# State-space stage: a kernel table padded in device memory, Toeplitz pieces loaded as overlapping rows, half of a table and the late decays moved

## The chip, the cores and the metric

The kernel runs on one core of one Trainium2 chip. The metric is the time of one execution on the device in microseconds (us). The core has TensorE (PE; its weight loads are shown as PEld), VectorE (DVE), ScalarE (ACT), GpSimd (POOL) and SyncE (SP). SP and ACT each have a queue from which they start DMA transfers; all transfers run on 16 DMA engines.

## The reference, cut to what matters

The program is a small encoder: a state-space (S5) layer, a gated MLP, a differential-attention layer, another gated MLP. Only the state-space layer is touched. In each of 64 groups of 16 channels a 64-dimensional complex diagonal state runs over 512 positions:

```python
lb_re, lb_im = mag * jnp.cos(dimg), mag * jnp.sin(dimg)
ht_re = hl_re + pw_re * hp_re - pw_im * hp_im
ht_im = hl_im + pw_re * hp_im + pw_im * hp_re
y = (jnp.einsum("btgp,gcp->btgc", ht_re, cr) - jnp.einsum("btgp,gcp->btgc", ht_im, ci))
y = y + d_skip.astype(f32) * u32
z = jax.nn.gelu(y).astype(u.dtype)
val, gate = jnp.split(z @ w_glu, 2, axis=-1)
return val * jax.nn.sigmoid(gate)
```

## The kernel before

The kernel is written engine by engine: one function for SP, POOL, ACT, DVE and PE each, with semaphores between them, so the order on an engine is the order of the code. The state-space layer splits the 512 positions into 64 blocks (NB) of 8 (BL). The output of a block is a part from within the block, a Toeplitz matrix of the kernel values k[0] to k[7] times the inputs, and a part carried in from the states at the block's start. The work is done in four pieces (OCTS) of 16 groups.

- `kx` holds the kernel values, one row of 8 KB per (piece, input channel), in partitions 32·piece to 32·piece+15. PE computes them in `kernel_rows`, ACT copies them out (L743), POOL adds the skip term to k[0] (L573) and signals `k_ready`.
- `toep[piece]` (1 MB each) holds, in partitions 16·lag to 16·lag+15, the kernel shifted right by 7−lag taps with zeros in front. `load_toeplitz` fills it from SBUF to SBUF with eight DMAs of 16 to 128 KB on SP's queue (L324); the zeros come from POOL's memsets (L571 for pieces 0 and 1, L576 for 2 and 3), which signal `toep_clear`. Pieces 2 and 3 lie where `ada_raw` buffers were, so their memsets wait until all 24 units of `ada_raw` are used (`ada_used`).
- PE's order at the end of the layer is `carried(0)`, `inputs(2)`, three `ada_raw` units, `carried(1)`, `inputs(3)`, `local(0)`, `local(1)`, `back(0)`, `carried(2)`, `local(2)`, `back(1)`, `local(3)`, `back(2)`, `carried(3)`, then the first unit of the gated projection (L2038), `back(3)` in its midst. `local` (L1926) multiplies by `toep`, `carried` (L1941) by the carried states `hx`, `back` (L1952) transposes the activated tile `z`, `inputs` is L1910.
- ACT's order there is `z_steps(0)`, `copy_row(2)`, `z_steps(1)`, `zt_steps(0)`, a weight split, `zt_steps(1)`, `z_steps(2)`, `zt_steps(2)` and so on. `z_steps` (L761) is the gelu of a piece and needs its `local` and `carried`; `zt_steps` (L771) copies what `back` wrote.
- DVE forms `hx` piece by piece: products with the rotation tables `rot_c`, `rot_s`, two scans that read a `decay` tile (L1392, L1393), and six operations that end in L1408, signalling `hx_im`. POOL fills the second half of the rotation tables (L532 to L541) and all four decay tiles (L556, L557).
- SP also issues on the same queue: 24 loads of `ada_raw` (L404, 1 MB each) before the Toeplitz loads, `raw` (L415, the weights of the next stage, 1 MB) after pieces 1 and 3, and `x` (L418, 2 MB).

Of the kernel before, what the change touches and what calls it, by code (L numbers as in the profile page):

```python
# [17 lines left out]
F32 = mybir.dt.float32  # L18
F32R = mybir.dt.float32r
I32 = mybir.dt.int32  # L20
ALU = mybir.AluOpType
ACT = mybir.ActivationFunctionType
AXX = mybir.AxisListType.X

P = 128
D = 1024
SEQ = 512
KT = D // P
# [6 lines left out]
CG = 16  # L35
GROUPS = D // CG
PAIRS = GROUPS // 2
BL = 8
NB = SEQ // BL
OCTS = 4  # L40
PO = PAIRS // OCTS
# [19 lines left out]
N_ADA_PE = 3 * KT  # L61
# [15 lines left out]
def build(nc, a, out_rows):  # L77

    ctx = ExitStack()
    with ctx:  # L80
# [14 lines left out]
        def sem(name):  # L95
            return ctx.enter_context(nc.semaphore(name))
# [3 lines left out]
        raw = at("raw", [P, 2, UNIT], F32, raw_at)  # L100
# [35 lines left out]
        toep = []  # L136
# [14 lines left out]
        for i in range(2):  # L151
# [60 lines left out]

        raw_landed = [sem("raw_landed0"), sem("raw_landed1")]
# [24 lines left out]
        k_psum, k_copied, k_ready, toep_clear = (sem("k_psum"), sem("k_copied"), sem("k_ready"),  # L238
                                                 sem("toep_clear"))
# [80 lines left out]
        def load_toeplitz(eng, piece):  # L320

            eng.wait_ge(toep_clear, piece + 1)
            for lag in range(BL):
                eng.dma_start(toep[piece][CG * lag:CG * (lag + 1), BL - 1 - lag:, :, :],  # L324
                              kx[32 * piece:32 * piece + CG, 0:lag + 1, :, :]).then_inc(toep_in[piece], 16)
# [66 lines left out]
        def _(sp):  # L392
# [17 lines left out]
            for piece in range(OCTS):  # L410
                load_toeplitz(sp, piece)
                if piece % 2:
                    n = piece // 2
                    sp.wait_ge(ada_used, 20 + n)
                    sp.dma_start(raw[:, n, :], a["units"][n]).then_inc(raw_landed[n], 16)  # L415
# [62 lines left out]
        def _(pool):  # L478
# [11 lines left out]
            nc.gpsimd.memset(ones[:], 1.0).then_inc(const_ready, 1)  # L490
            nc.gpsimd.memset(col[:, 0:1], 1.0 / D).then_inc(const_ready, 1)
# [69 lines left out]
            cosines(32, slice(2 * PO, PAIRS), cb[:, 1, :])  # L561
            sines(32, slice(2 * PO, PAIRS), cb[:, 1, :])
            pool.sem_inc(rot_ready, 1)
# [5 lines left out]
            pool.wait_ge(ada_used, 2 * KT)  # L569
            for i in range(2):  # L570
                nc.gpsimd.memset(toep[i][:], 0.0).then_inc(toep_clear, 1)  # L571
            pool.wait_ge(k_copied, 4)
            nc.gpsimd.tensor_tensor(kx[:, 0], kx[:, 0], tk, ALU.add).then_inc(k_ready, 1)  # L573
            for piece in range(2, OCTS):
                pool.wait_ge(ada_used, N_ADA_PE)
                nc.gpsimd.memset(toep[piece][:], 0.0).then_inc(toep_clear, 1)  # L576
                decay_tile(piece)
# [79 lines left out]
        def _(act):  # L657
# [51 lines left out]

            def scaled(piece, quarter):  # L710

                act.wait_ge(u_normed, piece + 1)
                g0 = 2 * PO * piece + 4 * quarter
                for g in range(g0, g0 + 4):
                    ins = A(u[:, g, :], u[:, g, :], ACT.Identity, scale=uab[:, g:g + 1],
                            bias=uab[:, GROUPS + g:GROUPS + g + 1])
                if quarter == 3:
                    ins.then_inc(u_ready, 1)
# [8 lines left out]
            lb_first(3)  # L727
            copy_inputs(2)
# [13 lines left out]
            for b in range(4):  # L742
                A(kx[:, :, 4 * b:4 * b + 4, :].rearrange("p k j c -> p j k c"),  # L743
                  psum[:, 3 + b, :].rearrange("p (j k c) -> p j k c", j=4, k=BL),
                  ACT.Copy).then_inc(k_copied, 1)
            for quarter in range(4):
                scaled(3, quarter)

# [345 lines left out]
        def _(dve):  # L1094
# [570 lines left out]
            dve.wait_ge(pos_in, 16 * BL + 16)  # L1665
# [5 lines left out]
            dve.wait_ge(lam_in, 16 * BL + 16)  # L1671
# [151 lines left out]
        def _(pe):  # L1823
# [58 lines left out]
            pe.wait_ge(lb_zero, 4)  # L1882
# [36 lines left out]
            def local(piece, first=True):  # L1919

                pe.wait_ge(toep_in[piece], 16 * BL)
# [634 lines left out]
```

## Time and profile before

| | |
|---|---|
| median of three runs | 1231.02 us (1229.38 to 1232.24) |
| the profiled execution | 1231.23 us, of which the trace spans 1229.4 us |
| busy in the span | PE 1191.3 us, DVE 748.0, ACT 517.7, POOL 390.7 |
| chain that ended last | 85% PE, 7% DVE, 2% ACT, 1% SP's queue |

PE is busy for 97% of the span, so what can be gained or lost lies in the few stretches in which PE stands still, and in its clock. A "wait" is idle time just ahead of an instruction, put down to what released it. The landing time of a DMA is from its issue to the semaphore that says it has arrived. The state-space stage ends at about 141 us; everything after it follows from PE's end of that stage.

### The profile page before, as it was taken

The page shows a single profiled execution, that of the slowest core. Times are in us where ns is not written, and L with a number is a line of the kernel's source. Part 1 is how long each engine was busy: PE and PEld are TensorE (multiplying, and loading weights), DVE is VectorE, ACT ScalarE, POOL GpSimd, SP SyncE. Part 2 cuts the span into 40 slices and gives each one's busy share as a digit, 9 for nine tenths or more (in the row PEclk, how much of TensorE's full clock was granted, in tenths as well). Part 3 has the DMA queues.
Part 4 walks back from the last instruction along what each step waited for, and adds up shares of the span by engine and source line. Part 5 has one row for each costly group of instructions (what it writes and reads, how often), then busy time and mean ns, then how long its engine had stood idle before and what let it go on. Part 6 is the DMA issues. An engine that isn't in the chain of part 4 may idle for free.

```text
span 1229.4 us, 17450 instructions
## 1 busy us (share of the span) xinstructions
PE 1191.3 (97%) x6420; PEld 955.4 (78%) x6420; DVE 748.0 (61%) x987; ACT 517.7 (42%) x789; POOL 390.7 (32%) x270
## 2 busy tenths in 40 slices
PE   5988999999999999999999999999999999999998
PEld 1757888778888887888788777677788888878887
DVE  7998787889964543242873778866744444442323
ACT  3373444253343343141432677755444334442311
POOL 4972100355653433000213453510443444330000
PEclk9989999999999999999999999999999999999999
DMA  9768635356732223223133222311222222223221
GB/s 369 297 272 156 257 147 204 119 220 216 285 148 103 102 78 129 103 90 116 49 115 114 88 78 87 88 49 69 71 100 102 102 102 95 80 98 137 78 94 69
DMA packets 26697, 162.19 MB, mean 132 GB/s; under 512 B 4497, under 2 KB 4817, under 8 KB 8401
## 3 DMA queue, kind: packets, MB, share of 16 engines
q1 hardware_dynamic: 25632, 161.15, 37.2%
q8 instruction: 37, 0.61, 0.2%
q10 hardware_dynamic: 1008, 0.28, 0.1%
q14 instruction: 20, 0.16, 0.0%
HBM read 152.76 MB, written 2.10 MB: 126 GB/s over the span
## 4 chain that ended last, share of the span: by engine, by line
PE 85%; DVE 7%; issue 2%; ACT 2%; POOL 1%; SPq 1%; DMA 0%; ACTq 0%; DVEq 0%; POOLq 0%
PE psum L2004 17%; PE psum L2006 17%; PE psum L2005 17%; PE psum L2268 3%; PE psum L2270 3%; PE psum L2269 3%; PE psum L2168 3%; PE psum L2169 3%; PE psum L2170 3%; PE psum L1872 2%; PE psum L2329 1%; PE psum L1833 1%; PE psum L2350 1%; PE psum L2317 1%; SPq L324 1%
## 5 line engine op out<-in xcount | busy, mean ns | idle before, releaser
L2004 PE MATMUL psum<-hhi,whi 128*128 128x512 f32 x896 | 352.2, 393 | 0.5 <-DVE wlo L1354 0.5
L2006 PE MATMUL psum<-hhi,wlo 128*128 128x512 f32 x896 | 348.9, 389 | 0.0
L2005 PE MATMUL psum<-hlo,whi 128*128 128x512 f32 x896 | 348.8, 389 | 0.0
L1354 DVE TENSOR_TENSOR wlo<-raw,whi 128x2048 fp32r<-128x2048 f32 x81 | 192.4, 2376 | 174.5 <-ACT whi L754 174.5
L754 ACT ACTIVATE whi<-raw 128x2048 fp32r<-128x2048 f32 x80 | 153.2, 1915 | 164.4 <-PE psum L2270 76.4
L594 POOL TENSOR_TENSOR ca<-ca,cb 128x512 f32<-128x512 f32 x44 | 141.5, 3216 | 231.7 <-ACT ca L900 231.7
L2004 PEld LDWEIGHTS psum<-hhi,whi 128*128 128x128 f32 x896 | 168.5, 188 | 38.5 <-issue 2.1
L2006 PEld LDWEIGHTS psum<-hhi,wlo 128*128 128x128 f32 x896 | 168.2, 188 | 35.5
L2005 PEld LDWEIGHTS psum<-hlo,whi 128*128 128x128 f32 x896 | 168.3, 188 | 33.8
L1552 DVE SCALAR_TENSOR_TENSOR ca<-psum,convp,ca 128x511 f32<-128x511 f32 x44 | 33.0, 749 | 199.3 <-ACT ca L896 199.3
L902 ACT ACTIVATE ghi<-ca 128x512 f32 (+1 forms) x44 | 27.8, 632 | 154.3 <-POOL ca L594 154.3
L896 ACT ACTIVATE ca<-psum,convp 128x512 f32<-128x512 f32 x44 | 34.2, 778 | 122.7 <-PE psum L2006 115.2
L596 POOL TENSOR_TENSOR glo<-ca,ghi 128x512 f32 (+1 forms) x44 | 67.8, 1542 | 41.3 <-ACT ghi L902 41.3
L584 POOL TENSOR_TENSOR stat<-nwt,power 128x4 f32<-128x4 f32 x6 | 6.4, 1069 | 228.9 <-DVE nwt L1483 224.9
L2168 PE MATMUL psum<-whi,ghi 128*128 128x512 f32 x176 | 68.8, 391 | 0.8 <-DVE wlo L1354 0.8
L2268 PE MATMUL psum<-ghi,whi 128*128 128x512 f32 x176 | 68.6, 390 | 0.7 <-DVE wlo L1354 0.7
L2170 PE MATMUL psum<-whi,glo 128*128 128x512 f32 x176 | 68.5, 389 | 0.0
L2269 PE MATMUL psum<-glo,whi 128*128 128x512 f32 x176 | 68.5, 389 | 0.0
L2169 PE MATMUL psum<-wlo,ghi 128*128 128x512 f32 x176 | 68.5, 389 | 0.0
L2270 PE MATMUL psum<-ghi,wlo 128*128 128x512 f32 x176 | 68.5, 389 | 0.0
L1421 DVE SCALAR_TENSOR_TENSOR ada_acc<-ada_ring,cond,ada_acc 128x2048 f32<-128x2048 f32 x24 | 62.4, 2601 | 0.0
L988 ACT ACTIVATE prob<-psum,stat 128x128 f32<-128x128 f32 (+3 forms) x64 | 33.1, 523 | 17.9 <-DVE stat L1692 17.6
(397 smaller groups left out, 1886.4 us busy)
## 6 DMA issues: line engine op xcount, KB each, us to landing
raw<-in_units SPq DMA_DIRECT2D x92, 1024.0 KB, 4.8
ada_raw<-in_ada_w SPq DMA_DIRECT2D x24, 1024.0 KB, 7.3
ada_ring<-in_ada_w SPq DMA_DIRECT2D x24, 1024.0 KB, 4.8
qk_sw<-ca SPq DMA_DIRECT2D x32, 128.0 KB, 2.3
u<-in_x_blocks SPq DMA_DIRECT2D x1, 2048.0 KB, 10.1
x<-in_x_t SPq DMA_DIRECT2D x1, 2048.0 KB, 10.1
out_rows<-y_late SPq DMA_DIRECT2D x8, 256.0 KB, 2.1
bc_par<-in_s_bc SPq DMA_DIRECT2D x1, 1024.0 KB, 5.5
```

What stands on the lines that cost most here:

```text
L594: nc.gpsimd.tensor_tensor(ca[:, s, :], ca[:, s, :], cb[:, s, :], ALU.mult).then_inc(g_ready, 1)
L754: A(whi[:, s, :], raw[:, s, :], ACT.Copy).then_inc(split_hi, 1)
L1354: TT(wlo[:, s, :], raw[:, s, :], whi[:, s, :].bitcast(F32), ALU.subtract).then_inc(split_lo, 1)
L2004: M(out, w_hi, hi[:, k, :], start=(k == 0), stop=False)
L2005: M(out, w_hi, lo[:, k, :], start=False, stop=False)
L2006: return M(out, w_lo, hi[:, k, :], start=False, stop=(k == KT - 1))
L2168: M(out, ghi[:, row, tok], whi[:, s, w], start=(isinstance(v, int) and row == 0), stop=False)
L2169: M(out, ghi[:, row, tok], wlo[:, s, w], start=False, stop=False)
L2170: return M(out, glo[:, row, tok], whi[:, s, w], start=False, stop=(isinstance(v, int) and row == JT - 1))
L2268: M(out, whi[:, s, w], ghi[:, row, :], start=(fixed and row == 0), stop=False)
L2269: M(out, whi[:, s, w], glo[:, row, :], start=False, stop=False)
L2270: return M(out, wlo[:, s, w], ghi[:, row, :], start=False, stop=(fixed and row == JT - 1))
```

## The change

1. A table `kpad` in device memory has one row per (piece, input channel), 15 taps of 1 KB. ACT writes the first 7 taps of all 64 rows as zeros with four DMAs (L753 of the changed kernel) from `ssum`, which POOL clears at the start.
2. When `k_ready` comes, SP stores the four pieces of `kx` behind the zeros, four DMAs of 128 KB (L416), and waits for all eight (`kpad_in`).
3. Each Toeplitz piece is then one 1 MB load from `kpad` (L328): row (lag, channel) starts lag taps into the channel's row and is 8 taps long, so rows overlap. POOL's four memsets of `toep` are gone.
4. SP's order becomes: four stores, pieces 0 and 1, both `raw` loads, a wait for `ada_used` 24, pieces 2 and 3.
5. POOL does two products of the rotation table's second half ahead, with `ssum` as scratch instead of `cb`, then waits for `hx_im` of piece 0 and does the other four operations, and only then the addition that gives `k_ready`.
6. The decay tiles of pieces 2 and 3 are made by ACT (`decay_late`), around `scaled(3)`.

```diff
+        K_TAP = 2 * PO * CG
+        K_ROW = (2 * BL - 1) * K_TAP
+        kpad = nc.dram_tensor("kpad", (OCTS * CG, K_ROW), F32, kind="Internal")
+        kpad_rows = kpad.ap()
...
         def load_toeplitz(eng, piece):
 
-            eng.wait_ge(toep_clear, piece + 1)
-            for lag in range(BL):
-                eng.dma_start(toep[piece][CG * lag:CG * (lag + 1), BL - 1 - lag:, :, :],
-                              kx[32 * piece:32 * piece + CG, 0:lag + 1, :, :]).then_inc(toep_in[piece], 16)
+            eng.dma_start(toep[piece][:].rearrange("p k q c -> p (k q c)"),
+                          bass.AP(kpad, CG * piece * K_ROW, [[K_TAP, BL], [K_ROW, CG], [1, BL * K_TAP]])
+                          ).then_inc(toep_in[piece], 16)
...
             sp.wait_ge(k_ready, 1)
             for piece in range(OCTS):
+                sp.dma_start(kpad_rows[CG * piece:CG * piece + CG, (BL - 1) * K_TAP:],
+                             kx[32 * piece:32 * piece + CG].rearrange("p k q c -> p (k q c)")
+                             ).then_inc(kpad_in, 16)
+            sp.wait_ge(kpad_in, 16 * (4 + OCTS))
+            for piece in range(2):
                 load_toeplitz(sp, piece)
-                if piece % 2:
-                    n = piece // 2
-                    sp.wait_ge(ada_used, 20 + n)
-                    sp.dma_start(raw[:, n, :], a["units"][n]).then_inc(raw_landed[n], 16)
+            for n in range(2):
+                sp.wait_ge(ada_used, 20 + n)
+                sp.dma_start(raw[:, n, :], a["units"][n]).then_inc(raw_landed[n], 16)
+            sp.wait_ge(ada_used, N_ADA_PE)
+            for piece in range(2, OCTS):
+                load_toeplitz(sp, piece)
...
             decay_tile(0)
             decay_tile(1)
-            cosines(32, slice(2 * PO, PAIRS), cb[:, 1, :])
-            sines(32, slice(2 * PO, PAIRS), cb[:, 1, :])
-            pool.sem_inc(rot_ready, 1)
+            half = slice(2 * PO, PAIRS)
+            oc, os, ic, is_, em_c, em_s, t = rotation(32, half, ssum)
+            pool.wait_ge(kpad_in, 16 * 4)
+            nc.gpsimd.tensor_tensor(oc, ic, em_c, ALU.mult).then_inc(pool_step, 1)
+            nc.gpsimd.tensor_tensor(t, is_, em_s, ALU.mult).then_inc(pool_step, 1)
...
-            pool.wait_ge(ada_used, 2 * KT)
-            for i in range(2):
-                nc.gpsimd.memset(toep[i][:], 0.0).then_inc(toep_clear, 1)
+            pool.wait_ge(hx_im, 1)
+            link(nc.gpsimd.tensor_tensor(oc, oc, t, ALU.subtract))
+            sines(32, half, ssum)
+            pool.sem_inc(rot_ready, 1)
             pool.wait_ge(k_copied, 4)
             nc.gpsimd.tensor_tensor(kx[:, 0], kx[:, 0], tk, ALU.add).then_inc(k_ready, 1)
-            for piece in range(2, OCTS):
-                pool.wait_ge(ada_used, N_ADA_PE)
-                nc.gpsimd.memset(toep[piece][:], 0.0).then_inc(toep_clear, 1)
-                decay_tile(piece)
...
+            def decay_late(piece):
+
+                act.wait_ge(decay_ready, piece)
+                act.wait_ge(scanned, piece - 1)
+                dst, mag = decays[piece % 2], s5s[:, 18, PO * piece:PO * piece + PO]
+                A(dst[:, :, 1:], mag.unsqueeze(2).broadcast_to([P, PO, NB - 1]), ACT.Copy)
+                A(dst[:, :, 0], mag, ACT.Copy, scale=0.0).then_inc(decay_ready, 1)
...
+            act.wait_ge(lb_zero, 5)
+            for lo in range(0, (BL - 1) * K_TAP, SEQ):
+                n = min(SEQ, (BL - 1) * K_TAP - lo)
+                act.dma_start(kpad_rows[:, lo:lo + n], ssum[0:OCTS * CG, 0:n]).then_inc(kpad_in, 16)
```

In the order of the built program, SP's queue before, from the last Toeplitz DMAs of piece 1 on (`toep_76` is piece 1, `toep_77` piece 2):

```order
L324 DMA toep_76<-kx 16x1792
L324 DMA toep_76<-kx 16x2048
L415 DMA raw<-in_units 128x2048 [waits ada_used]
L324 DMA toep_77<-kx 16x256 [waits toep_clear]
L324 DMA toep_77<-kx 16x512
```

SP's queue in the changed kernel, from `k_ready` to the load of `x`:

```order
L416 DMA kpad<-kx 16x2048 [waits k_ready]
L416 DMA kpad<-kx 16x2048 x3
L328 DMA toep_75<-kpad 128x1x2048 [waits kpad_in]
L328 DMA toep_76<-kpad 128x1x2048
L424 DMA raw<-in_units 128x2048 [waits ada_used] x2
L328 DMA toep_77<-kpad 128x1x2048 [waits ada_used]
L328 DMA toep_78<-kpad 128x1x2048
L430 DMA x<-in_x_t 128x8x512 [waits hx_im,hx_re]
```

Thirty-two small DMAs have become four stores and four loads, and both `raw` loads now stand ahead of pieces 2 and 3. The printed shape of a DMA is that of its destination; the source of L328 has the shape 8x16x2048.

POOL before, from the second half of the rotation tables to its last decay tile:

```order
L532 TENSOR_TENSOR rot_c<-rot_c 128x16x31
L533 TENSOR_TENSOR cb<-rot_s 128x496 [waits pool_step]
L534 TENSOR_TENSOR rot_c<-rot_c,cb 128x16x31 [waits pool_step]
L539 TENSOR_TENSOR rot_s<-rot_c,rot_s 128x16x31 [waits pool_step]
L540 TENSOR_TENSOR cb<-rot_s,rot_c 128x496 [waits pool_step]
L541 TENSOR_TENSOR rot_s<-rot_s,cb 128x16x31 [waits pool_step]
L567 TENSOR_TENSOR cb<-sel_96,dskip 128x256 [waits pool_step,sel_ready,small_in]
L571 MEMSET toep_75 128x2048 [waits ada_used,pool_step]
L571 MEMSET toep_76 128x2048
L573 TENSOR_TENSOR kx<-kx,cb 128x256 [waits k_copied]
L576 MEMSET toep_77 128x2048 [waits ada_used]
L556 COPY decay<-s5s 128x512 [waits scanned]
```

POOL in the changed kernel, the same stretch:

```order
L577 TENSOR_TENSOR rot_c<-rot_c 128x16x31 [waits kpad_in]
L578 TENSOR_TENSOR ssum<-rot_s 128x496
L584 TENSOR_TENSOR cb<-sel_96,dskip 128x256 [waits sel_ready,small_in,pool_step]
L587 TENSOR_TENSOR rot_c<-rot_c,ssum 128x16x31 [waits hx_im,pool_step]
L552 TENSOR_TENSOR rot_s<-rot_c,rot_s 128x16x31 [waits pool_step]
L553 TENSOR_TENSOR ssum<-rot_s,rot_c 128x496 [waits pool_step]
L554 TENSOR_TENSOR rot_s<-rot_s,ssum 128x16x31 [waits pool_step]
L591 TENSOR_TENSOR kx<-kx,cb 128x256 [waits pool_step,k_copied]
L616 MEMSET ada_acc 128x2048 [waits zt_psum]
```

Four of the six operations on the rotation tables now stand between the wait for `hx_im` and the addition to `kx`.

## Rows read from the trace of the kernel before

**Rows 1.** The page's first line.
```profile
span 1229.4 us, 17450 instructions
```
**Rows 2.** Waits of PE, 78 to 130 us: total, times, longest (us).
```profile
PE psum L1964 <- issue: 3.6, 1, 3.6
PE psum L1926 <- DMA toep<-kx: 3.3, 1, 3.3
PE psum L1952 <- ACT sq L696: 1.4, 1, 1.4
```
**Rows 3.** The chain that ended last: start us, us, what.
```profile
114.83 4.36 DMA toep<-kx
119.24 3.43 PE psum L1926 x32
...
123.84 3.64 PE psum L1941 x64
```
**Rows 4.** Timeline of PE: start us, us, line, operation, idle before.
```profile
103.26 3.67 PE L1926 MATMUL psum<-toep,u 128*64 128x128 f32 x64
108.28 1.06 PE L1952 MATMUL psum<-ident,z 128*128 128x128 f32 x8 [1.36 <-ACT sq L696]
...
112.92 1.97 PE L1926 MATMUL psum<-toep,u 128*64 128x128 f32 x32
```
**Rows 5.** Windows: stretch, us, busy by engine (PE first), PEclk, DMA share, GB/s.
```profile
119.20:123.00 3.80, 3.76 (x34) 3.44 (x35) 0.29 (x1) 0.00 (x0) 0.00 (x0) 0.55 0.81 281
```
**Rows 6.** Windows around the `kernel_rows`, same columns.
```profile
80.00:83.60 3.60, 0.00 (x0) 0.00 (x0) 3.46 (x4) 0.06 (x1) 3.30 (x3) 0.78 1.01 419
83.60:89.00 5.40, 5.39 (x106) 2.58 (x106) 5.20 (x9) 2.55 (x6) 2.67 (x3) 0.52 0.46 190
```
**Rows 7.** Timeline of POOL, same columns as PE's.
```profile
74.67 1.16 POOL L534 TENSOR_TENSOR rot_c<-rot_c,cb 128x496 f32<-128x496 f32 x1
...
78.83 1.94 POOL L541 TENSOR_TENSOR rot_s<-rot_s,cb 128x496 f32<-128x496 f32 x1
...
88.59 0.73 POOL L573 TENSOR_TENSOR kx<-kx,cb 128x256 f32<-128x256 f32 x1 [2.73 <-ACT kx L743]
```
**Rows 8.** Timeline of DVE, pieces 0 and 1.
```profile
76.31 1.53 DVE L1389 TENSOR_TENSOR v_ni<-v_ni,ca 128x512 f32<-128x512 f32 x1
77.87 1.95 DVE L1392 TENSOR_TENSOR_SCAN v_re<-decay,v_re 128x512 f32<-128x512 f32 x1
...
85.33 0.68 DVE L1408 TENSOR_TENSOR hx<-hx,ca 128x504 f32<-128x504 f32 x1
...
90.51 1.22 DVE L1392 TENSOR_TENSOR_SCAN v_re<-cb,v_re 128x512 f32<-128x512 f32 x1
...
96.17 0.68 DVE L1408 TENSOR_TENSOR hx<-hx,ca 128x504 f32<-128x504 f32 x1
```
**Rows 9.** SP's DMAs of L324: issue ns min/median/max; then landing times.
```profile
L324 SPq DMA_DIRECT2D toep<-kx x32: 589/590/1609, 89.3 to 114.8; - x32
...
DMA to landing us min/median/max: 2.1/3.5/5.6
```
**Rows 10.** DMA issues of the whole span: count, KB each, median us to landing.
```profile
out_rows<-y_late SPq DMA_DIRECT2D x8, 256.0 KB, 2.1
...
toep<-kx SPq DMA_DIRECT2D x4, 128.0 KB, 4.3
```
**Rows 11.** SP's DMAs of L404 (1 MB each): landing times.
```profile
DMA to landing us min/median/max: 4.7/7.3/19.3
```
**Rows 12.** Timeline of ACT.
```profile
52.17 0.60 ACT L703 ACTIVATE inb_re<-psum 128x512 f32<-128x512 f32 x1 [4.46 <-PE psum L1872]
...
105.27 1.28 ACT L761 ACT_TABLE_LOAD   x1 [11.49 <-PE psum L1926]
...
117.76 1.13 ACT L761 ACTIVATE z<-psum 128x512 f32<-128x512 f32 x2
```
**Rows 13.** Waits of PE from 141 us on, the longest.
```profile
PE psum L2341 <- DVE att L1707: 2.2, 3, 1.6
```

More of the change, by code:

```diff
@@ L237, in build @@
         inb_psum, inb_ready = sem("inb_psum"), sem("inb_ready")
-        k_psum, k_copied, k_ready, toep_clear = (sem("k_psum"), sem("k_copied"), sem("k_ready"),
-                                                 sem("toep_clear"))
+        k_psum, k_copied, k_ready, kpad_in = (sem("k_psum"), sem("k_copied"), sem("k_ready"),
+                                                 sem("kpad_in"))
         usq_ready, usq_summed = sem("usq_ready"), sem("usq_summed")
@@ L490, in _ @@
             nc.gpsimd.memset(ones[:], 1.0).then_inc(const_ready, 1)
+            nc.gpsimd.memset(ssum[:], 0.0).then_inc(lb_zero, 1)
             nc.gpsimd.memset(col[:, 0:1], 1.0 / D).then_inc(const_ready, 1)
@@ L560, in _ @@
             decay_tile(1)
-            cosines(32, slice(2 * PO, PAIRS), cb[:, 1, :])
-            sines(32, slice(2 * PO, PAIRS), cb[:, 1, :])
-            pool.sem_inc(rot_ready, 1)
+            half = slice(2 * PO, PAIRS)
[3 more added lines that the diff above has]
+            nc.gpsimd.tensor_tensor(t, is_, em_s, ALU.mult).then_inc(pool_step, 1)
+            steps[0] += 2
+            pool.wait_ge(pool_step, steps[0])
             pool.wait_ge(small_in, 16 * 6)
@@ L745, in _ @@
                   ACT.Copy).then_inc(k_copied, 1)
+            decay_late(2)
             for quarter in range(4):
                 scaled(3, quarter)
+            decay_late(3)
             def split_high(n, s, half):
@@ L1664, in _ @@
             split_low(U_V + 2, 0, None)
-            dve.wait_ge(pos_in, 16 * BL + 16)
+            dve.wait_ge(pos_in, 32)
             ang, rt = prob[:, 0, 0, :], prob[:, 0, 1, :]
@@ L1670, in _ @@
             signal(rope_arg)
-            dve.wait_ge(lam_in, 16 * BL + 16)
+            dve.wait_ge(lam_in, 32)
             lp = prob[:, 1, 0, 0:2 * HD].rearrange("p (a d) -> p a d", a=2)
@@ L1880, in ada_units @@
                     ada_unit(n)
-            pe.wait_ge(lb_zero, 4)
+            pe.wait_ge(lb_zero, 5)
             ada_units(3, 5)
@@ L1919, in local @@
             def local(piece, first=True):
-                pe.wait_ge(toep_in[piece], 16 * BL)
+                pe.wait_ge(toep_in[piece], 16)
                 if first:
```

## The prediction

> **What bounds the kernel now.** I read the share of the span first: PE works nearly all of the 1229.4 us [rows 1], so only the stretches in which PE stands still can give time, or a new one of that kind can cost it. PE's waits are the second view: in the state-space stage there are three, 3.6 us without a releaser in `kernel_rows` (L1964), 1.4 us for ACT ahead of `back(0)`, and 3.3 us for the Toeplitz DMAs [rows 2]. The change is about the last one. The third view, the chain in order of time, shows where it stands: the last DMA of piece 3 is issued at 114.83, lands at 119.19, `local(3)` starts at 119.24, and `carried(3)` at 123.84 [rows 3]. That 123.84 is my yardstick, since from `carried(3)` on PE's order is unchanged and its largest wait for one releaser in all the rest is 2.2 us in total [rows 13], none of them tied to a fixed time: what the start of `carried(3)` gains or loses, the end of the program should gain or lose.
>
> The wait costs more than itself. `local(3)` takes 3.43 us for 32 records [rows 3], `local(2)` 1.97 for the same 32 [rows 4], and the granted clock from 119.2 to 123.0 is 0.55 [rows 5], which is mostly the lower of the two levels. PE had stood still for 3.3 us just before.
>
> **What goes.** POOL's four memsets, the eight small DMAs of each piece and their 0.59 us of issue each [rows 9] go: pieces 2 and 3 no longer wait for 16 issues after `ada_used`. The landing of piece 3 is what the change replaces by another time, which I now work out step by step.
>
> **When `kx` is ready.** Before, POOL's addition ends at 88.59 + 0.73 = 89.3 [rows 7]. Now POOL waits for `hx_im` of piece 0 first, which came at 85.33 + 0.68 = 86.0, and has four operations on 496 columns to do behind it. They would end the addition at about 92.4. But DVE also gets faster: from its first scan to that `hx_im` piece 0 took 8.1 us (77.87 to 86.01), piece 1 only 6.3 (90.51 to 96.85), the scan itself 1.95 against 1.22 [rows 8]. Piece 0 ran while POOL was in the rotation tables, piece 1 did not. With POOL standing still I take off 1.8 us, and 1 us for the additions ahead of the scan (1.53 us for one of them), so `hx_im` comes at 83.2. POOL's four operations take 1.16 us alone and up to 1.94 beside DVE [rows 7]; between the two, with the steps between them, 6.1 us, then 0.8 for the addition: `k_ready` at 90.1. Bounds: 89.3 (nothing lost, ACT's copy of `kx` sets it) and 92.5 (DVE gains nothing). Behind this wait on POOL stands only the addition; DVE needs the second half of the tables for piece 2 alone, after 96.
>
> **The stores.** The first of four starts at `k_ready`, the last three issues of 0.59 later, 1.8 us. The trace has no store of 16 rows of 8 KB to device memory. The nearest rows: 256 KB from 128 partitions to device memory lands in 2.1 us, 128 KB out of the same 16 partitions of `kx` into SBUF in 4.3 [rows 10], the slowest Toeplitz DMA in 5.6 [rows 9]. I take 4.3, because the source is the same, and 2.1 and 5.6 as bounds. All stores have landed 6.1 us after `k_ready` (3.9 to 7.4): T = 96.2.
>
> The Trainium skill speaks of this step too (DMA: Bandwidth & Descriptors, Anatomy of one DMA): about 2.0 us fixed plus the bytes over 436 GB/s, most of it the receipt from the target, device memory being the slow one. By it the last store would land 2.3 us after its issue, T would be 94.2 and the end 2 us earlier than below; the row of 4.3 us disagrees for SBUF to SBUF, and none here shows a store of this shape.
>
> **The four loads.** At full share the DMA engines moved 419 GB/s [rows 6], so 1 MB of data takes 2.5 us on sixteen engines. The fastest 1 MB load landed in 4.7 us [rows 11], which leaves 2.2 us beside the data. The queue order is piece 0, piece 1, `raw`, `raw`, piece 2, piece 3. Their source is new in one point: its outermost dimension counts 8 lags, with 16 channels and 2048 contiguous elements inside. Every other load and store, the old 16-row ones too, has 16, 32, 64 or 128 outermost on both sides. If a transfer is dealt out to the DMA engines along its outermost dimension, this one can use eight engines, and its 1 MB takes 5.0 us instead of 2.5. No row decides it; the bounds are 2.5 and 5.0. I take 5.0: a dealing by outermost counts needs no reordering of the pattern, and 8 does not split in 16.
>
> The Trainium skill states such a rule (DMA: Bandwidth & Descriptors, Why a DMA increments its semaphore by 16 and not by 1): a DMA uses the largest number of engines up to 16 that divides the slowest dimension of both sides. By that rule it is eight here, and the end is that of the forecast; no transfer in this trace tests it.
>
> Engines that serve a piece also carry their share of `raw`. So on eight engines piece 0 lands at T + 2.2 + 5.0 = 103.4, piece 1 at 108.4, the two `raw` at 110.9 and 113.4, piece 2 at 118.4, piece 3 at 123.4. `ada_used` 24 holds nothing: PE uses the last `ada_raw` unit before `carried(1)` and `local(0)`, so before 103.26 [rows 4], long before piece 2 comes to the head of the queue.
>
> **What PE does with that.** `local(0)` started at 103.26 and `local(1)` halfway in the 3.67 us, at 105.1 [rows 4]. Piece 0 is just in time; `local(1)` waits 3.3 us. It runs 1.9 to 3.4 us (full or low clock), `back(0)` 1.0, `carried(2)` 3.6: PE is at `local(2)` by about 115 to 117 and waits until 118.4. Through `local(2)` (1.9 to 3.4) and `back(1)` (1.0) it is at `local(3)` by 121.3 to 122.8 and waits until 123.4. Then `local(3)` and `back(2)` take 2.8 us at full clock, 4.6 as before at low (119.24 to 123.84). `carried(3)` starts at 126.2 to 128.0, against 123.84: 2.4 to 4.2 us later. ACT's `z_steps(2)`, two half-microsecond steps at 117.76 [rows 12] behind `zt_steps(1)`, moves with `back(1)` and ends by 124.5 to 126, not later than PE. I take 3.2 us.
>
> **What costs nothing.** The zero rows: ACT's four issues (0.6 each at most by [rows 9], 2.4 in all) fall into the 4.46 us that ACT stood idle before 52.17 [rows 12]; without that cover 2.4 us would go onto ACT's copies that PE waits for. ACT's late decays, under 1 us each, fall between its `scaled` steps and the 11.49 us idle before 105.27 [rows 12]; uncovered they would delay DVE's scans of pieces 2 and 3. The clearing of `ssum` is under the start-up. POOL's tail after `k_ready` is now empty, which can only help DVE. The load of `x` can come to stand behind piece 3 by a few us; ACT reads it only after the first unit of the gated projection.
>
> **The sum.** The profiled execution took 1231.23 us, 1.8 more than its span, and the median of the runs is 1231.02, 0.2 below it. 1231.0 + 3.2 = 1234.2 us.
>
> **Rivals.**
> - *Sixteen engines: faster.* If the new source is spread as the others, the six loads take 2.5 us each: piece 0 at T + 4.7 = 100.9, piece 1 at 103.4, piece 2 at 110.9, piece 3 at 113.4, all ahead of PE. `local(3)` then starts when PE is free, at 119.24 − 3.3 = 115.9, takes 1.9, and `back(2)` waits 1.1 us for `z_steps(2)`, which ends at 118.9 [rows 12]. A wait of 1.4 us did not slow the 1.97 us of `local(2)` behind it [rows 2, 4], so the clock should hold. `carried(3)` starts at 119.9, 3.9 us earlier: 1227.1 us. For it: every 1 MB load so far came at full rate. Against: none has 8 outermost. It decides from piece 3 landing before 115.9.
> - *Eight engines, but fast stores: no change.* With stores of 2.1 us T is 94.0; piece 3 lands at 121.2 and `carried(3)` starts at 124.0 to 125.8, 0.2 to 2.0 us later: about 1232.1 us. For it: the only store to device memory took 2.1 us. Against: it read 128 partitions. It holds up to T = 95.4, where the middle of the range reaches 2.5 us.
> - *A stall like that of `kernel_rows`.* There PE stood for 3.6 us with no releaser while the DMA engines were at full share, and the clock was then 0.52 for 5.4 us, which costs another 2.6 [rows 2, 6]. The new loads keep eight or sixteen engines full from 97 to 113 or 121. If PE's instruction supply suffers from it, 3 to 6 us are added to either case, partly inside the new waits: about 1237 us, or 1232 with sixteen engines.
>
> **How the numbers follow.** Eight engines with stores near the row of 4.3 us, the forecast: 0.43. Eight engines with fast stores: 0.25. Sixteen engines: 0.26. The stall: 0.06. A measurement tells about 0.2%, 2.5 us, from no change: faster is below 1228.6, slower above 1233.5. The forecast case spans 1233.4 to 1235.2 by the clock alone, with `k_ready` at its bounds 1232.6 to 1237.6, and its own range is 1232.5 to 1237. Nearly all of it is slower, all of the second case is no change, all of the third is faster. That gives faster 0.26, same 0.30, slower 0.44. The range has to reach into the third case, since it holds more than 0.2: from 1226.8 to 1237.0.
>
> **What the profile after would show.** The number of engines: the landing of L328, 4.7 to 5.5 us for piece 0 if sixteen, over 7 if eight, and a DMA share near one half between 98 and 105 while a piece loads alone. `k_ready`: the end of L591, near 90. The stores: L416 to landing. PE's waits at `toep` in three places instead of one, and the low clock behind them. DVE's scans of piece 0 near 1.2 us. I am wrong if the pieces land ahead of PE, if PE's wait moves to ACT (`back(2)`), or if DVE's piece 0 does not get faster.

## The result, and the profile after

The changed kernel is slower: median 1258.91 us (1256.99 to 1259.90, 4 runs) against 1230.20 us (1228.34 to 1232.24, 4 runs) of the kernel before on the same chip, ratio 1.0227, 95% interval 1.0211 to 1.0242. The prediction said 1234.2 us with a range up to 1237.0. The direction was right, the size was not: 28.7 us came instead of 3.2.

The first view is again the span with PE's busy time (span; engine, us, share).

```profile
span 1256.2 us, 17428 instructions
...
PE   1199.7 (96%) x6420; PEld 962.9 (77%) x6420; DVE 745.8 (59%) x987; ACT 518.9 (41%) x793; POOL 379.6 (30%) x263
```

The span grew by 26.8 us. PE's waits from 78 to 166 us of the changed kernel, which answer to [rows 2], say where:

```profile
PE psum L1954 <- DMA toep<-kpad: 24.1, 4, 8.4
PE psum L1992 <- issue: 3.3, 1, 3.3
```

One wait of 3.3 us for the Toeplitz table has become four of 24.1 us. PE's timeline of the changed kernel (start, duration, line; in brackets the idle time ahead and its releaser) places them, beside [rows 3, 4]:

```profile
110.71 3.68 PE L1954 MATMUL psum<-toep,u 128*64 128x128 f32 x32 [8.39 <-DMA toep<-kpad]
122.16 3.68 PE L1954 MATMUL psum<-toep,u 128*64 128x128 f32 x32 [7.77 <-DMA toep<-kpad]
...
136.52 3.68 PE L1954 MATMUL psum<-toep,u 128*64 128x128 f32 x32 [5.01 <-DMA toep<-kpad]
140.13 1.80 PE L1980 MATMUL psum<-ident,z 128*128 128x128 f32 x8
144.87 3.56 PE L1954 MATMUL psum<-toep,u 128*64 128x128 f32 x32 [2.94 <-DMA toep<-kpad]
148.36 1.12 PE L1980 MATMUL psum<-ident,z 128*128 128x128 f32 x8
149.40 1.96 PE L1969 MATMUL psum<-cl_re,hx 64*64 64x128 f32 x32
```

The four rows of L1954 are `local(0)` to `local(3)`, each released by its piece of the table, so their starts are the landings: 110.7, 122.2, 136.5 and 144.9. `carried(3)` starts at 149.40, 25.6 us later than at 123.84 [rows 3]; the yardstick explains all but 1.2 us of the longer span. Each `local` also takes 3.56 to 3.68 us, instead of the 1.97 that `local(2)` took before [rows 4].

The windows view of the changed kernel (stretch, length, busy us and records of PE, PEld, DVE, ACT, POOL, then granted clock, DMA share, GB/s) shows the DMA engines at work:

```profile
98.00:102.00 4.00, 4.00 (x104) 3.83 (x100) 3.84 (x6) 0.00 (x0) 0.00 (x0) 1.00 0.87 164
102.00:110.00 8.00, 0.32 (x12) 0.18 (x7) 7.73 (x13) 0.00 (x0) 0.00 (x0) 0.84 1.04 160
...
120.00:126.00 6.00, 3.84 (x33) 3.51 (x34) 0.00 (x0) 0.00 (x0) 0.00 (x0) 0.50 0.93 326
126.00:132.00 6.00, 5.50 (x72) 4.93 (x71) 0.00 (x0) 4.14 (x7) 0.00 (x0) 0.84 0.53 120
132.00:140.00 8.00, 3.48 (x32) 3.28 (x32) 0.00 (x0) 0.57 (x1) 0.00 (x0) 0.67 0.50 116
```

The last row is the key: while only a table piece is being moved, the share is 0.50, which is that of eight engines, and they move 116 GB/s. Eight engines at the rate of [rows 6] would move 210. Between 102 and 110, with the `raw` loads beside them, all sixteen are busy and move only 160 GB/s. The clock from 120 to 126 us is 0.50, the lower level (1.2 of 2.4 GHz); PE stood still for the 7.8 us before 122.16, and `local(1)` then ran at that level.

### The profile page after: what moved, and what is told of

Read it like the earlier page. It is cut to its first block, busy times and chain, and to the rows that moved or that the text cites. A ratio compares the mean times of both kernels' runs of the same rounds, so it can differ in the third digit from the quotient of the medians.

```text
span 1256.2 us, 17428 instructions
## 1 busy us (share of the span) xinstructions
PE 1199.7 (96%) x6420; PEld 962.9 (77%) x6420; DVE 745.8 (59%) x987; ACT 518.9 (41%) x793; POOL 379.6 (30%) x263
## 4 chain that ended last, share of the span: by engine, by line
PE 79%; DVE 11%; DMA 4%; issue 2%; POOL 1%; ACT 1%; SPq 0%; ACTq 0%; DVEq 0%; POOLq 0%
PE psum L2032 17%; PE psum L2034 16%; PE psum L2033 16%; DMA toep<-kpad 4%; PE psum L2296 3%; PE psum L2297 3%; PE psum L2298 3%; PE psum L2196 3%; PE psum L2197 3%; PE psum L2198 3%; PE psum L2357 1%; PE psum L2378 1%; PE psum L2345 1%; PE psum L2066 1%; PE psum L2339 1%
```

## The experiments

The runs were made on several chips, so each time stands beside the median of the kernel before on the same chip; the runs of that kernel spread over 6 to 7 us on a chip, and no finer difference should be read from a time of one run. Four questions were asked: is it the number of engines, the overlap of the rows, or the order in which partitions are written; what do the `raw` loads between the pieces cost; what is the table worth if its loads run at full rate; and what are the moves on POOL and ACT worth.

### Channels outermost in the source

```diff
-                          bass.AP(kpad, CG * piece * K_ROW, [[K_TAP, BL], [K_ROW, CG], [1, BL * K_TAP]])
+                          bass.AP(kpad, CG * piece * K_ROW, [[K_ROW, CG], [K_TAP, BL], [1, BL * K_TAP]])
```

> The four loads keep their 128 overlapping rows of 8 KB from the same table, but the source pattern has the 16 channels outermost and the 8 lags inside, so the rows land in another order of partitions: the output of the state-space layer is not the reference's. Theory A, only the outermost count of 8 is at fault (eight DMA engines at work, each also slow): sixteen engines work, a load takes about 2.5 us of data, all pieces have landed by 113, PE waits for none, and the time is 1226 to 1229 us. Theory B, the overlapping rows are at fault (many engines read the same few KB of device memory): a packet stays at 0.6 to 0.9 us, loads take 5 to 10 us, and the time stays 10 us or more above before. Theory C, the table's place in device memory or its fresh writing is at fault: as B.

Measured: 1239.87 us (one run; before 1232.17). In the windows view of this kernel:

```profile
100.00:104.00 4.00, 4.00 (x90) 3.83 (x86) 3.87 (x6) 0.00 (x0) 0.00 (x0) 1.00 0.98 217
```

With 16 outermost the share is 0.98 instead of one half: the outermost count does set the number of engines. But sixteen engines move 217 GB/s, half of the 419 of [rows 6]. So a second thing halves the rate of each engine, here as there. Against its own kernel before this one loses 7.7 us instead of 28.7. That lies between the theories: A had expected no loss, B and C ten or more.

### Rows without overlap, eight and sixteen outermost

```diff
-                          bass.AP(kpad, CG * piece * K_ROW, [[K_TAP, BL], [K_ROW, CG], [1, BL * K_TAP]])
+                          a["units"][8 + piece].rearrange("(c l) e -> l c e", l=BL)
```

> The four loads keep the outermost count of 8 with 16 rows of 8 KB inside, but read 128 rows that do not overlap, from weight units instead of the table: the Toeplitz pieces hold weights, so the output is not the reference's. Theory A (outermost count): DMA share and rate stay at about one half and 110 to 120 GB/s while a piece loads alone, and the time stays at about 1258 us. Theory B (overlap): the rate goes to 210 GB/s on eight engines or 420 on sixteen, pieces land in 5 to 7 us each, time 1227 to 1236 us. If both play a part: half the engines at full rate each, pieces at 5 us each, time about 1234 us.

Measured: 1256.24 us (one run; before 1232.17), PE waits 24.7 us for the table in four places. The waits and a window of this kernel:

```profile
PE psum L1954 <- DMA toep<-in_units: 24.7, 4, 8.7
```

```profile
104.00:108.00 4.00, 0.00 (x0) 0.00 (x0) 3.83 (x8) 0.00 (x0) 0.00 (x0) 0.87 1.01 160
```

The same 160 GB/s beside `raw`, and nearly the same waits (24.7 against 24.1 us), without any overlapping row and from another place in device memory, so theories B and C are out. The loss is 24.0 us against 28.7; with one run that difference can't be read. The counterpart with 16 outermost:

```diff
+                          a["units"][8 + piece].rearrange("(l c) e -> c l e", l=BL)
```

> As rows8 (weights instead of the table in the Toeplitz pieces, so the output is not the reference's), but the source pattern has 16 outermost and 8 rows of 8 KB inside; no rows overlap. The run with overlapping rows and 16 outermost moved 217 to 227 GB/s while a piece loaded, at 0.6 us for an 8 KB packet, half of what plain loads do. Theory P (ports of SBUF: sixteen engines each walk a block of 8 neighbouring partitions in step, so that two of them always write through the same port): the rate stays at 215 to 230 GB/s, time as then, 1238 to 1242 us. Theory B (the overlap costs the rest): without it the rate is 380 to 425 GB/s, time 1226 to 1230 us.

Measured: 1237.71 us (one run; before 1232.25), and in its windows view

```profile
100.00:104.00 4.00, 3.76 (x98) 3.45 (x96) 3.88 (x6) 0.00 (x0) 0.00 (x0) 1.00 0.98 213
```

213 GB/s against the 217 of the overlapping rows, and a loss of 5.5 us against 7.7: overlap costs nothing here either (the time is 0.3 us under the band of theory P). What is left for the half rate is the order in which rows are read and the partitions that are written at the same time; the run with eight engines below separates the two.

### One DMA for each lag, sixteen partitions each

```diff
-            eng.dma_start(toep[piece][:].rearrange("p k q c -> p (k q c)"),
-                          bass.AP(kpad, CG * piece * K_ROW, [[K_TAP, BL], [K_ROW, CG], [1, BL * K_TAP]])
-                          ).then_inc(toep_in[piece], 16)
+            for lag in range(BL):
+                eng.dma_start(toep[piece][CG * lag:CG * (lag + 1)].rearrange("p k q c -> p (k q c)"),
+                              bass.AP(kpad, CG * piece * K_ROW + lag * K_TAP, [[K_ROW, CG], [1, BL * K_TAP]])
+                              ).then_inc(toep_in[piece], 16)
```

> Each piece is loaded from the same table by eight DMAs of 16 rows of 8 KB, one for each lag, outermost count 16 on both sides, 16 destination partitions each. Theory A: sixteen engines work, and if the destination does not matter a piece takes 2.5 us of data plus eight issues of 0.4 to 0.6 us, about 4 us, all landed by about 117: time 1228 to 1231 us. If 16 partitions at a time are a limit of their own (the old transfers between 16 and 16 partitions moved 94 GB/s), a piece takes about 10 us, and the time is 1245 us or more. Theory B (overlapping source): a DMA's own rows do not overlap but those in flight together do, so slow as after.

Measured: 1243.02 us (one run; before 1232.17). Its windows view:

```profile
100.00:104.00 4.00, 2.21 (x68) 1.95 (x64) 3.88 (x6) 0.00 (x0) 0.00 (x0) 1.00 1.03 139
```

All sixteen engines are busy and together move 139 GB/s into 16 neighbouring partitions. So engines can be kept busy by the place that they write to, with nothing wrong in their number. The time is 2 us under the 1245 that was expected if 16 partitions are a limit.

### Eight engines, thirty-two partitions at a time

```diff
+            for q in range(4):
+                eng.dma_start(toep[piece][32 * q:32 * q + 32].rearrange("p k q c -> p (k q c)"),
+                              a["units"][8 + piece, 32 * q:32 * q + 32].rearrange("(c l) e -> l c e", l=BL)
+                              ).then_inc(toep_in[piece], 16)
```

> As rows8 (weights in the Toeplitz pieces, output not the reference's), outermost count 8, but each piece in four DMAs onto 32 neighbouring partitions each, 4 rows for each of the eight. Theory P: still eight engines, but each now walks its own 4 partitions and no two share a port, so an 8 KB packet takes 0.31 us instead of 0.56 to 0.6 while a piece loads alone, the rate is near 210 GB/s at a DMA share near one half, a piece takes 5 us: about what the prediction took for eight engines, time 1232 to 1238 us. Rival (eight engines are slow by themselves, whatever the destination): the packets stay at 0.6 us, rate 115 GB/s, time near 1256 us.

Measured: 1241.56 us (one run; before 1232.25), and in its windows view

```profile
98.00:102.00 4.00, 4.00 (x84) 3.83 (x82) 3.86 (x5) 0.00 (x0) 0.00 (x0) 1.00 0.51 205
...
104.00:108.00 4.00, 1.49 (x28) 1.24 (x24) 3.83 (x7) 2.41 (x4) 0.00 (x0) 1.00 1.01 293
...
112.00:116.00 4.00, 3.66 (x33) 3.33 (x33) 3.83 (x6) 0.00 (x0) 0.00 (x0) 0.50 0.51 213
```

Eight outermost again and a share of one half again, but 205 to 213 GB/s instead of 116 to 120. The same eight engines run at full rate once their blocks are 4 partitions apart instead of 16. By their shapes they also read the same rows in the same order as in the run with eight outermost above, so neither the reading nor the number of engines makes the half rate: the partitions written do. The time missed its expected upper end of 1238 by 3.6 us. Piece 1 stands ahead of `raw` in the queue and still landed only at 112.3: `raw`, issued at 101.65, took the eight free engines, and from 104 to 108 all sixteen moved 293 GB/s, not 419. The expectation was right on the rate of a piece alone and too low on what `raw` costs it.

The packet records of the same traces show it for one packet of 8 KB (from 98 to 102 us; in the changed kernel from 136 to 139 us, where only a table piece is being moved; in the kernel before from 80 to 83.6 us, [rows 6]):

```
kernel                          median ns of one 8 KB packet   GB/s
kernel before, plain loads      309                            419
changed kernel, pieces alone    622                            112
sixteen outermost, no overlap   608                            233
one DMA for each lag            945                            135
blocks of 4, eight outermost    309                            205
```

### The table tap by tap

The table is laid out with the tap slowest, so the source's outermost dimension can count all 128 rows (lag and channel together), with 8 taps of 1 KB inside. The stores and the zero rows follow the new layout.

```diff
-                          bass.AP(kpad, CG * piece * K_ROW, [[K_TAP, BL], [K_ROW, CG], [1, BL * K_TAP]])
+                          bass.AP(kpad, piece * K_PIECE, [[K_TAP, BL * CG], [CG * K_TAP, BL], [1, K_TAP]])
```

> The table is laid out tap by tap (tap, channel, 256 values), so that row (lag, channel) starts 1 KB behind the row before it: the load's source has 128 outermost, 8 chunks of 1 KB inside. Same result as the reference. Theory A: sixteen engines, 1024 packets of 1 KB, about 3 us of data for a piece, all landed by 115, PE's waits for the pieces gone: time 1226 to 1229 us. Theory B (overlap of rows read together): packets slower than alone, a piece in 5 us or more, time 1235 us or more. Theory C (place or fresh writing): as B.

Measured: median 1229.21 us (10 runs) against 1232.17 (13 runs), ratio 0.9975, interval 0.9963 to 0.9987. Its windows view:

```profile
104.00:108.00 4.00, 3.64 (x68) 3.30 (x62) 3.83 (x7) 2.08 (x3) 0.00 (x0) 1.00 1.03 389
```

With 128 on both sides the engines move 389 GB/s, `raw` and the 1 KB chunks of the table together, and the change is a small gain instead of a loss of 29 us. The expected 1229 us was missed by 0.2, and PE's waits did not vanish: it still waited 2.2 us for the table.

### The same with one raw load between the pairs

```diff
-            for n in range(2):
-                sp.wait_ge(ada_used, 20 + n)
-                sp.dma_start(raw[:, n, :], a["units"][n]).then_inc(raw_landed[n], 16)
+            sp.wait_ge(ada_used, 20)
+            sp.dma_start(raw[:, 0, :], a["units"][0]).then_inc(raw_landed[0], 16)
...
+            sp.dma_start(raw[:, 1, :], a["units"][1]).then_inc(raw_landed[1], 16)
```

> The tap-by-tap table (128 outermost in the load's source), with SP's order changed to pieces 0 and 1, first raw load, pieces 2 and 3, second raw load. The tap-by-tap run waited 1.9 us for piece 2 and then had ACT as the limit at the second transpose after 1.2 us. If the queue order is what made piece 2 late, that wait shrinks to under 0.5 us and the time falls by 0.5 to 1.5 us more, to 0.995 to 0.998 of before. If ACT's z_steps(2) decides anyway, nothing changes against that run.

Measured: median 1227.37 us (1227.13 to 1228.11, 5 runs) against 1232.25 (15 runs), ratio 0.9962, interval 0.9948 to 0.9976: the fastest kernel measured here. PE's waits from 78 to 166 us, and two rows of its timeline:

```profile
PE psum L1980 <- ACT sq L710: 1.4, 1, 1.4
PE psum L1980 <- ACT z L789: 1.2, 1, 1.2
```

```profile
117.88 1.09 PE L1980 MATMUL psum<-ident,z 128*128 128x128 f32 x8 [1.16 <-ACT z L789]
118.91 1.96 PE L1969 MATMUL psum<-cl_re,hx 64*64 64x128 f32 x32
```

No wait for the table is left; ACT's gelu sets `back(2)`, as in the rival with sixteen engines, and `carried(3)` starts at 118.91. The expected ratio was 0.995 to 0.998.

### The moves on POOL and ACT alone, and the table alone

The kernel before with only steps 5 and 6 of the change:

```diff
-                decay_tile(piece)
...
+            decay_late(2)
             for quarter in range(4):
                 scaled(3, quarter)
+            decay_late(3)
```

> The kernel before with only the moves on POOL and ACT: the second half of the rotation tables behind hx_im of piece 0, the decay tiles of pieces 2 and 3 on ACT; Toeplitz loads and memsets as before. If the moves are neutral on the path, k_ready stays at 89 to 90 and the last Toeplitz DMA still lands at 119, no measurable change (0.998 to 1.002). If freeing POOL and DVE matters by itself, pieces 2 and 3 start up to 1 us earlier because POOL no longer makes decay tiles between its memsets: 1 us faster. If the later k_ready matters, up to 1 us slower.

Measured: median 1231.77 us (11 runs) against 1232.25 (15 runs), ratio 0.9998, interval 0.9986 to 1.0009. And the other way round, the fastest kernel without steps 5 and 6:

```diff
+            for piece in range(2, OCTS):
+                decay_tile(piece)
...
-            decay_late(2)
-            decay_late(3)
```

> The best kernel so far (tap-by-tap table, raw loads between the pairs of table loads) without the moves on POOL and ACT: the rotation table's second half stands where it stood before the change, and the decays of pieces 2 and 3 are made on POOL again. Theory (the moves are worth nothing by themselves, because the two pieces before the kernel table are paced by ACT and DVE): same time as with them, 1226.5 to 1229.5 us, and carried(3) starts within 0.7 us of 118.9 us. Rival (the moves free the shared port for DVE and let the kernel table be ready earlier): the table is ready 1 to 2 us later without them, and the time is 1228.5 to 1230 us.

Measured: median 1227.73 us (12 runs) against 1230.47 (17 runs), ratio 0.9978, interval 0.9968 to 0.9988. POOL's addition, whose end is `k_ready`, in this kernel:

```profile
90.23 0.72 POOL L583 TENSOR_TENSOR kx<-kx,cb 128x256 f32<-128x256 f32 x1 [7.70 <-ACT kx L755]
```

It ends at 90.95, against 89.19 in the changed kernel, and `carried(3)` starts at 120.78 instead of 118.91, outside the 0.7 us that the first theory allowed. That looks like the rival, but PE's timeline shows the difference already ahead of it. The first row of the second stretch of `kernel_rows` in this kernel:

```profile
80.14 0.43 PE L1976 MATMUL psum<-cl_re,kb 64*16 64x128 f32 x16
```

and in the fastest kernel:

```profile
78.30 0.43 PE L1992 MATMUL psum<-cl_re,kb 64*16 64x128 f32 x16
```

This execution was 1.8 us late before the table was begun, and stayed so. The moves don't make that difference: the kernel tap by tap, which has them, shows 79.91, and the kernel before, without them, 78.27. Counted from that row, `k_ready` comes after 10.8 us without the moves and 10.9 with them, `carried(3)` after 40.6 in both.

The medians decide less. 1227.73 is in the first theory's band and under the rival's, but the bands were set where the kernel before took 1232.25, and here it took 1230.47; the ratio of 0.9978 would make 1229.5 there, which lies at the edge of the first band and inside the rival's. The intervals of the fastest kernel (0.9948 to 0.9976) and of this one (0.9968 to 0.9988) overlap, with 2 us between their middles. So the table alone is a gain, the moves alone are worth nothing that can be measured, and beside the new table the traces show nothing for them, while the times leave up to some 2 us open.

### The raw loads behind all four pieces

```diff
-            for n in range(2):
-                sp.wait_ge(ada_used, 20 + n)
-                sp.dma_start(raw[:, n, :], a["units"][n]).then_inc(raw_landed[n], 16)
             sp.wait_ge(ada_used, N_ADA_PE)
             for piece in range(2, OCTS):
                 load_toeplitz(sp, piece)
+            for n in range(2):
+                sp.dma_start(raw[:, n, :], a["units"][n]).then_inc(raw_landed[n], 16)
```

> The changed kernel with the two raw loads issued behind the four table loads instead of between them; nothing else differs. Theory (engines paired on ports: a table load alone moves 115 GB/s and keeps eight engines busy, so 1 MB takes 9.1 us, and the raw rows between them cost the table about 8 us more): the pieces land 9.1 us apart from about 97.7 us, the fourth at about 134 us against 144.9 us, PE waits about 15 us for the table in all, and the time is 1247 to 1249 us. Rival (the order in the queues doesn't matter, since all engines stay busy to the same end): the fourth piece lands near 145 us as now and the time stays at 1257 to 1260 us.

Measured: 1258.53 us (one run; before 1230.47), as slow as the changed kernel (28.1 us lost against 28.7). The time is in the rival's range, but not for the rival's reason. Its PE timeline:

```profile
110.11 3.68 PE L1953 MATMUL psum<-toep,u 128*64 128x128 f32 x32 [7.72 <-DMA toep<-kpad]
...
139.69 1.97 PE L1953 MATMUL psum<-toep,u 128*64 128x128 f32 x32 [1.90 <-DMA toep<-kpad]
146.84 1.97 PE L1979 MATMUL psum<-ident,z 128*128 128x128 f32 x8 [5.18 <-ACT z L788]
148.74 3.48 PE L1968 MATMUL psum<-cl_re,hx 64*64 64x128 f32 x32
```

The fourth piece came by 139.7, 5 us earlier than in the changed kernel, where the theory had 11 and the rival none. The first still came only at 110.1, although nothing stood ahead of it. Its windows view shows why:

```profile
102.00:106.00 4.00, 0.40 (x14) 0.26 (x10) 3.80 (x7) 0.00 (x0) 0.00 (x0) 1.00 0.97 154
106.00:110.00 4.00, 0.00 (x0) 0.00 (x0) 3.93 (x7) 0.00 (x0) 0.00 (x0) 0.69 1.07 170
...
138.00:146.00 8.00, 1.97 (x32) 1.73 (x32) 0.93 (x2) 3.92 (x6) 0.00 (x0) 0.93 0.50 196
```

All sixteen engines are busy before the first piece has landed: the eight that have no table rows had begun `raw` at once, though it was issued last, and the packets of both took longer (median 0.88 us from 106 to 110, against 0.62 for a piece alone). The place in the queue didn't protect the table. The last row is a control within one execution: from 139.7 on the table is in place, the same eight engines move what they still had of the other loads, and at a share of 0.50 again they reach 196 GB/s.

What was won was lost again on ACT, whose timeline is

```profile
142.08 1.91 ACT L781 ACTIVATE whi<-raw 128x2048 fp32r<-128x2048 f32 x1 [13.25 <-DMA raw<-in_units]
143.90 1.98 ACT L798 ACTIVATE hhi<-psum 128x256 fp32r<-128x256 f32 x4
145.67 1.11 ACT L788 ACTIVATE z<-psum 128x512 f32<-128x512 f32 x2
```

and the chain that ended last has one row for all of it:

```profile
98.44 43.56 DMA raw<-in_units
```

`raw` landed at 142.0, the weight split stands ahead of `zt_steps(1)` and `z_steps(2)` on ACT, and `back(2)` waited 5.2 us for them. A late load of the next stage held this stage through ACT's order.

## Why the prediction was wrong

**The step that failed** is in "The four loads": "its 1 MB takes 5.0 us instead of 2.5", with 5.0 as the upper bound. The number of engines was right; the rate of each was taken as that of a plain load, and nothing in the sum held a factor for it. The changed kernel's six loads, 6.3 MB, were done 47.1 us after 97.7 (issue of the first plus the 2.2 us fixed), 133 GB/s; the prediction gave them 25.0. The last piece, alone, came 8.35 us behind the third (136.52 to 144.87), against 5.0. The waits that grew from it, 24.1 us in four places, are the loss.

The trace before held a warning that the prediction did not use. While the old Toeplitz DMAs alone were under way, from 16 partitions to 16, its windows view has

```profile
89.00:97.00 8.00, 8.00 (x153) 5.94 (x152) 7.65 (x11) 4.78 (x15) 0.32 (x1) 1.00 0.57 76
```

76 GB/s at a share of 0.57, where the plain loads of [rows 6] would have moved 236 at that share. Which side of the copy made it slow can't be told from there, but the rate of a busy engine was plainly not fixed.

**What is in its place.** The eight blocks of the source's outermost dimension are written to blocks of 16 neighbouring partitions. That each block has one engine, and that all walk their blocks in step, is inferred from the shape and the share; no record names an engine's partition. Those engines hinder one another: a packet takes 0.62 us instead of 0.31. The runs separate it from the rest. The overlap of rows is not at fault (160 GB/s with it and without it). The number of engines is a second, separate factor (share 0.50 with 8 outermost, 0.98 with 16). With the same eight engines, the same rows read and blocks of 4 partitions the half rate is gone (205 to 213 GB/s), and with sixteen engines in blocks of 8 it is there (213 and 217). That writes of several engines meet at a shared entrance to the memory of neighbouring or alike-numbered partitions is inferred from these rates; no record names such an entrance.

The Trainium skill describes such an entrance (SBUF — State Buffer, Door 1: The DMA port swizzle): DMA has 16 ports into SBUF, bits 2 to 4 and bit 6 of a partition's number choose the port, and the bandwidth depends on how many ports the partitions reach. To count only the ports of the partitions written at one moment, as is done next, is a step of this document. The eight engines start at partitions 0, 16, ... 112, which by that formula lie on 4 ports, an estimate of 109 GB/s as a quarter of the page's 436; blocks of 8 lie on 8 ports at a time, by the same estimate 218 GB/s; 32 partitions in blocks of 4 reach 8 ports, one an engine. These runs come near: 116, 213 to 217, and 205 to 213. One doesn't: the sixteen partitions of a lag lie on 4 ports too, and 139 GB/s went there.

**Right, by their rows.** `k_ready`, forecast at 90.1, and DVE's scans of piece 0 without POOL beside them: POOL and DVE of the changed kernel, against [rows 7, 8],

```profile
83.11 1.15 POOL L587 TENSOR_TENSOR rot_c<-rot_c,ssum 128x496 f32<-128x496 f32 x1 [7.81 <-DVE hx L1436]
...
88.23 0.96 POOL L591 TENSOR_TENSOR kx<-kx,cb 128x256 f32<-128x256 f32 x1 [0.18 <-ACT kx L769]
```

```profile
76.62 1.23 DVE L1420 TENSOR_TENSOR_SCAN v_re<-decay,v_re 128x512 f32<-128x512 f32 x1
...
82.28 0.68 DVE L1436 TENSOR_TENSOR hx<-hx,ca 128x504 f32<-128x504 f32 x1
...
86.97 1.63 DVE L1417 TENSOR_TENSOR v_ni<-v_ni,ca 128x512 f32<-128x512 f32 x1
```

The scan takes 1.23 us instead of 1.95, `hx_im` comes at 82.96 (forecast 83.2), and the table is ready at 89.19. The slow operations have moved to piece 1 (1.63 us for a subtraction that takes 0.68), where POOL now works beside DVE, and cost PE nothing.

The stores, forecast to have landed at 96.2: SP's issues in the changed kernel, against [rows 9],

```profile
89.22 3.08 SPq L416 DMA_DIRECT2D kpad<-kx  x4
95.53 1.40 SPq L328 DMA_DIRECT2D toep<-kpad  x2
```

The loads go out at 95.53. A store took 3.5 us at the median (2.9 to 3.9), between the bounds of 2.1 and 5.6 and below the 4.3 taken, but above the 2.3 with which the prediction tried another sum.

The zero rows cost nothing, as forecast: ACT is idle for the same 4.46 us behind them [rows 12].

```profile
52.29 0.60 ACT L717 ACTIVATE inb_re<-psum 128x512 f32<-128x512 f32 x1 [4.46 <-PE psum L1900]
```

ACT's late decays ended at 88.7 and 94.6, the second ahead of an idle time of 19.9 us. The yardstick held: +25.6 us at `carried(3)`, +26.8 in the span, +28.7 in the medians.

**A second, smaller miss.** The prediction looked for a share near one half from 98 to 105, "while a piece loads alone". It never was alone: the eight free engines took their rows of `raw` at once. This interference stood in no term of the sum. Between the first and second piece 11.5 us passed and between the second and third 14.4, against 8.35 for a piece by itself.

**The rivals.** Sixteen engines at full rate were priced at 1227.1, 3.9 us under the kernel before, with `carried(3)` at 119.9 and a wait of 1.1 us for `z_steps(2)`. The table tap by tap has that rate in the prediction's own order of loads: 1229.21, 0.25% or 3.1 us under its kernel before (interval 1.6 to 4.6), with piece 2 still late by 1.9 us. With one `raw` between the pairs it is 1227.37, 0.38% or 4.7 us under (interval 3.0 to 6.4), `carried(3)` at 118.91, the wait 1.16 us. So the rival's price was right to about 1 us. The stall like that of `kernel_rows` did not come: PE's only wait without a releaser is the old one of 3.3 us, and with the DMA share at 1.10 from 100 to 104 PE was busy throughout in the fastest kernel:

```profile
100.00:104.00 4.00, 4.00 (x104) 3.83 (x102) 3.88 (x6) 0.00 (x0) 0.00 (x0) 1.00 1.10 373
```

**What stays open.** How the time of a packet divides between two engines that meet is not shown, and so not why sixteen partitions took 139 GB/s and eight engines in blocks of 16 only 116. Nor is it settled whether the moves on POOL and ACT are worth up to 2 us beside a table that loads at full rate, since the two kernels were never timed on one chip.

## What to carry to other kernels

A DMA's shape has two prices beside its bytes: the outermost count set how many engines carried it here (8 or 16), and the partitions that those engines wrote at the same moment set how fast each was. Where no row of the profile shows a shape, the upper bound has to hold a factor for each; here the two together made 1 MB cost 8.35 us, more than three times the 2.5 us of a plain load. Lay a table out so that one dimension of 128 can be outermost on both sides, even if the contiguous piece shrinks from 8 KB to 1 KB.

Don't count on a queue's order between loads that use different sets of engines: the one issued last may run at once on engines that the first leaves free, and slow the first down. And ask of a load that is pushed back who stands behind its reader.

## What the runs showed that was not expected

- A transfer whose DMA share is 1.0 can be at a third of the rate: 139 GB/s at share 1.03 into 16 partitions. The share says that engines hold packets, not that they move bytes; the GB/s beside it has to be read too.
- Chunks of 1 KB to 128 partitions run nearly as fast as plain loads: in the windows view of the fastest kernel, 363 GB/s from 98 to 102 us, when mostly the first pair was under way, against the 419 of [rows 6].

```profile
98.00:102.00 4.00, 4.00 (x103) 3.83 (x100) 3.86 (x5) 0.00 (x0) 0.00 (x0) 1.00 1.07 363
```

- With such loads in front of it, the issue of a DMA itself takes long. In the fastest kernel SP needed 5.19 us for one `raw` load, against 0.93 us for two in the changed one. It cost nothing, since no one waited for SP.

```profile
97.97 4.17 SPq L328 DMA_DIRECT2D toep<-kpad  x2
102.19 5.19 SPq L427 DMA_DIRECT2D raw<-in_units  x1
```
